# Rotary embedding of a sparse attention: swapping half heads by transfers within SBUF instead of by a permutation on TensorE

## The reference, cut to what matters

```python
def apply_rope(x):                 # x: (b, s, heads, 64)
    half = d // 2
    c, sn = jnp.cos(ang), jnp.sin(ang)
    x1, x2 = x[..., :half], x[..., half:]
    return jnp.concatenate([x1 * c - x2 * sn, x1 * sn + x2 * c], axis=-1)

def dsa_attention(xn, w_in, w_o):
    q, k, v, qi, ki, wi = jnp.split(xn @ w_in, A_SPLITS, axis=-1)
    q, k, qi, ki = apply_rope(q), apply_rope(k), apply_rope(qi), apply_rope(ki)
    ...                            # index scores, top 64 keys, softmax, values
    return from_blocks(o) @ w_o
```

## Time and profile before

| | us |
|---|---|
| median of 3 runs | 1352.4 (1350.19 to 1352.61) |
| profiled execution, its own time | 1350.53 |
| its span, first to last instruction | 1348.8 |
| TensorE busy | 1303.3 (97%) |
| VectorE, ScalarE, GpSimd busy | 948.8, 701.5, 128.3 |
| granted TensorE clock, mean | 0.998 |

### The profile page before, as it was taken

The page is one execution under the profiler, slowest core; times in us unless marked ns, Lnnn a source line. Parts: engine busy times, 40 slices in busy tenths (PEclk is TensorE's granted clock), DMA queues, the critical chain, the costliest instruction groups (busy, mean ns, idle before and its releaser), DMA issues. The chain is left out here.

```text
span 1348.8 us, 24952 instructions
## 1 busy us (share of the span) xinstructions
PE 1303.3 (97%) x10507; PEld 1129.8 (84%) x10507; DVE 948.8 (70%) x1433; ACT 701.5 (52%) x1211; POOL 128.3 (10%) x133
## 2 busy tenths in 40 slices
PE   4999999999999999999999999999999999999997
PEld 2998888998899897788888887888888998888886
DVE  1887788976768776675566888666656677756655
ACT  2544544434567555564444648654445566644443
POOL 0000000010200764100000042000000021000000
PEclk9999999999999999999999999999999999999999
DMA  9996799995341012356665532465555543565561
GB/s 362 372 363 237 299 356 380 352 343 167 115 156 64 4 35 97 95 176 201 188 189 176 182 113 91 148 206 192 187 190 160 174 139 126 172 188 194 183 197 50
DMA packets 177575, 256.90 MB, mean 190 GB/s; under 512 B 10488, under 2 KB 122552, under 8 KB 177464
## 3 DMA queue, kind: packets, MB, share of 16 engines
q1 hardware_dynamic: 177464, 255.31, 56.8%
HBM read 254.25 MB, written 1.05 MB: 189 GB/s over the span
## 5 line engine op out<-in xcount | busy, mean ns | idle before, releaser
L1514 DVE TENSOR_TENSOR w_lo<-stage,w_hi 128x1024 fp32r<-128x1024 f32 (+1 forms) x372 | 447.6, 1239 | 160.4 <-ACT w_hi L889 160.0
L889 ACT ACTIVATE w_hi<-stage 128x1024 fp32r<-128x1024 f32 (+1 forms) x378 | 380.1, 1049 | 211.7 <-PE acc L2318 191.9
L2316 PE MATMUL acc<-w_hi,z_hi 128*128 128x512 f32 x640 | 252.6, 395 | 1.6 <-DVE z_lo L1963 1.6
L2318 PE MATMUL acc<-w_hi,z_lo 128*128 128x512 f32 x640 | 249.4, 390 | 0.0
L2317 PE MATMUL acc<-w_lo,z_hi 128*128 128x512 f32 x640 | 249.2, 389 | 0.0
L2259 PE MATMUL un<-h_both,w_hi 128*128 128x256 f32 x736 | 214.3, 291 | 1.8 <-POOL w_lo L860 1.1
L2260 PE MATMUL un<-h_both,w_hi 128*128 128x256 f32 x736 | 208.1, 283 | 0.0
L2261 PE MATMUL un<-h_both,w_lo 128*128 128x256 f32 x736 | 208.0, 283 | 0.0
L2259 PEld LDWEIGHTS un<-h_both,w_hi 128*128 128x128 f32 x736 | 140.8, 191 | 9.5 <-issue 5.4
L2316 PEld LDWEIGHTS acc<-w_hi,z_hi 128*128 128x128 f32 x640 | 120.1, 188 | 27.8 <-issue 4.0
L2260 PEld LDWEIGHTS un<-h_both,w_hi 128*128 128x128 f32 x736 | 141.0, 192 | 1.2 <-issue 0.7
(11 more groups left out here) (393 smaller groups left out, 1886.0 us busy)
## 6 DMA issues: line engine op xcount, KB each, us to landing
stage<-in_mlp_w SPq DMA_DIRECT2D x64, 1024.0 KB
ada_buf<-in_ada_w SPq DMA_DIRECT2D x48, 1024.0 KB, 11.4
stage<-in_w_up SPq DMA_DIRECT2D x32, 1024.0 KB
stage<-in_w_down SPq DMA_DIRECT2D x32, 1024.0 KB
stage<-in_conv_w_in SPq DMA_DIRECT2D x12, 1024.0 KB
stage<-in_rw_w_rkv SPq DMA_DIRECT2D x12, 1024.0 KB
stage<-in_w_in_a SPq DMA_DIRECT2D x8, 1024.0 KB
stage<-in_w_kv_b SPq DMA_DIRECT2D x8, 1024.0 KB
```

The source lines that it names most:

```text
L889: A_(w_hi[u % 2][:, half, 0:n], stage[u % NSTAGE][:, half, 0:n], ACT.Copy).then_inc(hi_made, 1)
L1514: V.tensor_tensor(w_lo[u % 2][:, half, 0:n], stage[u % NSTAGE][:, half, 0:n], w_hi[u % 2][:, half, 0:n].bitcast(F32), ALU.subtract).then_i ...
L2316: MM(y, z_hi[:, kt, q], wh[:, i, :], start=(first and kt == 0), stop=False, skip_group_check=True)
L2318: ins = MM(y, z_lo[:, kt, q], wh[:, i, :], start=False, stop=(last and kt == KT - 1), skip_group_check=True)
```

## The change

The permutation leaves TensorE. Behind its copy to rope_in ScalarE waits until the copy is done (it waits on un_free, which the copy itself raises) and issues four transfers within SBUF, each of 32 partitions, which write the swapped halves to a buffer of their own, rope_turned (two of them). DVE waits for the transfers instead of for the matmul. The sign of the swapped half moves into the table of sines. The constant matrix is replaced by an unused one of the same size. PE no longer waits for a rotation before it writes the banks of the last two query units. The mask of the selection is waited for over another semaphore, in the same place.

```diff
-               (("ident", P), ("mean", P), ("ones", P), ("rot", P)),
+               (("ident", P), ("mean", P), ("ones", P), ("still", P)),
...
-    put("sin", np.tile(np.sin(ang), (4, 1)))
+    put("sin", np.tile(np.sin(ang), (4, 1)) * np.where(i % HD < HD // 2, -1.0, 1.0)[:, None])
...
+        rope_turned = [at(f"rope_turned{i}", [P, 2, SEQ], tmp_off + 4096 + 2048 * i) for i in range(2)]
...
                 A_(rope_in[r % 2][:, 0:n, :], un[v % 2][:, 0:n, :], ACT.Copy, scale=scale).then_inc(un_free, 1)
+                act.wait_ge(un_free, freed(v))
+                for g in range(4):
+                    to, src = 32 * g, 32 * (g ^ 1)
+                    act.dma_start(rope_turned[r % 2][to:to + 32, 0:n, :], rope_in[r % 2][src:src + 32, 0:n, :]).then_inc(sem(f"rope_landed{r % 2}"), 16)
...
-            def rope(r, n, dst, bank=misc):
-                dve.wait_ge(rot_done, r + 1)
-                link(V.tensor_tensor(dst, bank[:, 0:n, :], bc4(sin_root, n), ALU.mult))
+            def rope(r, n, dst):
+                dve.wait_ge(sem(f"rope_landed{r % 2}"), 64 * (r // 2 + 1))
+                link(V.tensor_tensor(dst, rope_turned[r % 2][:, 0:n, :], bc4(sin_root, n), ALU.mult))
...
-            dve.wait_ge(rot_done, ROPE_KI + 1)
+            dve.wait_ge(wi_turned, 1)
...
-            V.tensor_scalar(sel_bias[:], score[:], 0.5 * TAKEN, NEG, ALU.is_gt, ALU.mult).then_inc(sem("keys_chosen"), 1)
-            dve.wait_ge(sem("keys_chosen"), 1)
+            link(V.tensor_scalar(sel_bias[:], score[:], 0.5 * TAKEN, NEG, ALU.is_gt, ALU.mult))
...
-            def rot(r, n, v):
-                pe.wait_ge(un_free, freed(v))
-                if r:
-                    pe.wait_ge(rope_done, r)
-                MM(misc[:, 0:n, :], rot_w, rope_in[r % 2][:, 0:n, :], start=True, stop=True).then_inc(rot_done, 1)
...
-                if k >= 7:
-                    pe.wait_ge(rope_done, ROPE_Q + k - 6)
...
-            rot(ROPE_KI, 1, V_A)
+            ins.then_inc(wi_turned, 1)
             a_unit(2)
-            rot(ROPE_QI, 2, V_A + 1)
             a_half(3, 0)
-            rot(ROPE_QI + 1, 2, V_A + 2)
             a_half(3, 1)
             index_scores(0)
             a_half(4, 0, tokens=True)
-            rot(ROPE_K, 2, V_A + 3)
             index_scores(1)
...
-            rot_query(0)
...
-            rot_query(1)
...
-                if p in (1, 3):
-                    rot_query(p // 2 + 2)
```

More of the change, by code:

```diff
@@ L45 @@
            "c", "final_g", "g_attn_a_2", "g_kv_2", "g_attn_b_2", "g_mlp_2", "g_final_2")
-CONST_PARTS = ((("ident", P), ("mean", P), ("ones", P), ("rot", P)),
+CONST_PARTS = ((("ident", P), ("mean", P), ("ones", P), ("still", P)),
                (("head_ones", P), ("head_mean", P), ("level_t", 6 * CHUNK), ("masks", 2 * CHUNK), ("eye", CHUNK), ("resets", SEQ),
@@ L76, in constant_table @@
     put("head_mean", same_head / HD)
[L77 to L81, removed]
     s, q = i[:, None] % CHUNK, np.arange(CHUNK)[None, :]
@@ L167, in c_ @@
             return const[i][:, lo - CONST_AT[i]:hi - CONST_AT[i]]
-        ident, mean_w, ones_w, head_ones, head_mean, rot_w = (c_(n) for n in ("ident", "mean", "ones", "head_ones", "head_mean", "rot"))
+        ident, mean_w, ones_w, head_ones, head_mean = (c_(n) for n in ("ident", "mean", "ones", "head_ones", "head_mean"))
         level_t = c_("level_t").rearrange("p (j q) -> p j q", j=6)
@@ L726, in build @@
                              "bonus_gated", "weighed", "scaled", "group_done", "last_done"))
-        rot_done, rope_done, ki_copied, cos_done, kdup_ready = (sem(n) for n in ("rot_done", "rope_done", "ki_copied", "cos_done", "kdup_ready"))
+        wi_turned, rope_done, ki_copied, cos_done, kdup_ready = (sem(n) for n in ("wi_turned", "rope_done", "ki_copied", "cos_done", "kdup_ready"))
         score_done, score_relu, score_used = sem("score_done"), sem("score_relu"), sem("score_used")
@@ L2158, in rope_query @@
             def rope_query(j):
-                rope(ROPE_Q + j, 2, q_fm[:, 2 * j:2 * j + 2, :], un[(V_A + 5 + j) % 2])
+                rope(ROPE_Q + j, 2, q_fm[:, 2 * j:2 * j + 2, :])
             rope_query(0)
             select(rounds - rounds // 2)
-            V.tensor_scalar(sel_bias[:], score[:], 0.5 * TAKEN, NEG, ALU.is_gt, ALU.mult).then_inc(sem("keys_chosen"), 1)
-            dve.wait_ge(sem("keys_chosen"), 1)
+            link(V.tensor_scalar(sel_bias[:], score[:], 0.5 * TAKEN, NEG, ALU.is_gt, ALU.mult))
             pair_logits(0, 0)
@@ L2844, in a_half @@
                     free_bank(V_A + k)
-                    if k >= 7:
-                        pe.wait_ge(rope_done, ROPE_Q + k - 6)
                 unit(U_KI + k, un[(V_A + k) % 2], h_tiles, tokens=tokens, kts=HALVES[n])
-            def rot_query(j):
-                v = V_A + 5 + j
-                pe.wait_ge(un_free, freed(v))
-                MM(un[v % 2][:], rot_w, rope_in[(ROPE_Q + j) % 2][:], start=True, stop=True).then_inc(rot_done, 1)
             def a_products(p):
@@ L2874, in _ @@
             for a in range(QT):
-                nc.tensor.transpose(misc[:, 1, IDX_HEADS * a:IDX_HEADS * (a + 1)], rope_in[ROPE_KI % 2][HD:KI_COLS, 0, P * a:P * a + P],
+                ins = nc.tensor.transpose(misc[:, 1, IDX_HEADS * a:IDX_HEADS * (a + 1)], rope_in[ROPE_KI % 2][HD:KI_COLS, 0, P * a:P * a + P],
                                     ident[HD:KI_COLS, HD:KI_COLS])
-            rot(ROPE_KI, 1, V_A)
+            ins.then_inc(wi_turned, 1)
             a_unit(2)
-            rot(ROPE_QI, 2, V_A + 1)
             a_half(3, 0)
-            rot(ROPE_QI + 1, 2, V_A + 2)
             a_half(3, 1)
```

## The result

The changed kernel takes 1367.24 us in the median of six runs (1364.57 to 1371.98), the kernel before, run beside it, 1351.06 us (1349.97 to 1352.61). The ratio is 1.0123, its 95% interval 1.0100 to 1.0146: 16.2 us slower, where the forecast said 5.7, and above the upper end of its range (1363.5). Why the six runs lie 7.4 us apart was not found.

The account below looks back on a forecast made before the run. ACT and DVE, not the 97% busy PE, were taken to have least room; +3.0 us up to q0's addition and +2.7 at q3 made +5.7, on 1350.5 to 1352.4 us: 1357.5 us predicted, range 1352.5 to 1363.5.

Parts of the forecast that it names:

- block of 1.9 us: At every rotation: four transfer issues (1.81 us, taken from SyncE's rows) plus ACT's wait for its copy cost ACT 1.9 us.
- landing of 2.1 us: Time from a transfer's issue to its landing, taken from stores out of SBUF: 2.1 us, hidden at most rotations.
- Rival A: PE's time counts: the removed 7.1 us of PE work are gained, 1343.4 us (1345.3 on the median); chance 0.08.
- B: Rival: issues cost ACT next to nothing, +1.0 us at q3, sum 0, 1350.5 to 1352.4 us; chance 0.12.
- +3.7: First step, rotations KI and QI: ACT's issues delay splits k = 2 and 3, so DVE's tables begin 3.7 us later.
- Step 2, QI+1: Rotation QI+1: copy waits for KI's rotation until 774.8 us; PE's index scores start 3.2 us later, PE idle about 3 us.
- gain of 0.8 us at QI: Rotation QI: without the permutation, DVE's addition waits only for POOL's product and starts 0.8 us earlier.
- Step 4, q0: Rotation q0: copy 2.1 us later, then transfers and landing; DVE's addition starts at 802.45 instead of 799.48 us, +3.0.
- Rival C: Transfers land late, at 4.1 us, as weight loads share the DMA engines: +10.2 us, 1361 to 1363 us; chance 0.20.
- Step 6, q3: Last query rotation, q3: copy to addition takes 5.2 instead of 2.53 us, as issues and landing are exposed: +2.7 us.
- Rival D: PE's idle 3 us before the index scores lowers its clock: +3 to +4 us on top, 1361 us; chance 0.07.
- Steps 3 and 5, the hidden ones: K's issues cost 0 in ACT's wait for index scores (cover 1.9 us left); q1's and q2's transfers are hidden too.

## Why the prediction was wrong

It had the direction and the mechanism: PE's time doesn't count, ACT and DVE have the least room, waits appear ahead of the index scores and at q3. It was wrong in size, by a factor of nearly three. What failed are two terms that it sized too small, ACT's block of 1.9 us for each rotation (3.1 us at KI, 2.7 at QI) and the landing of 2.1 us (5.5 us at q0, 3.7 at q3), and one that it left out of the sum, the low clock behind q3 (2.5 us). Step by step:

*What bounds the kernel.* Right. The kernel without permutations and transfers is not faster (1.0012), and the page's 97% was no bound here. Rival A is dead. So is B: the transfers that nobody reads, and the half number of them, show that the issues are the larger part. The kernel without transfers shows one thing more that no rival had: PE's idle time at q3 alone brings the clock down, for 1.6 us.

*The block of 1.9 us.* Too small. The forecast took four issues for 1.81 us by the earlier trace rows, loads of lora_g2b from memory, "since it has the shape". The transfers within SBUF take 2.44 us at best, 2.85 us at KI and 3.54 us at q0, where one issue of the four is long. At KI and QI this alone turns +3.7 into +5.6. The upper bound was missing: the nearest rows were taken as value and a smaller one as lower end, with nothing above.

*Step 2, QI+1.* The forecast had its copy wait for KI's rotation until 774.8 us. That rotation ended at 776.9 us, as the tables were late, and the copy waited 0.5 us more for PE: unit 2, started 2.9 us late and computed at 0.50 and 0.65 of the clock, gave the bank up at 777.39 us. So 2.1 of the 3.7 us by which +6.9 exceeds +3.2 are the block's size again, 0.5 is PE's clock, and most of the rest is QI+1's own block ahead of split k = 4. With PE kept busy the copy waits for KI's rotation, as forecast, and the index scores are no sooner for it. The gain of 0.8 us at QI was 0.2, because "I take no difference" between PSUM and SBUF was wrong while POOL works. That PE stood idle about 3 us there (2.9), as forecast, is luck in part: both ends of the wait were late, by 3.7 us and more.

*Step 4, q0.* +3.0 was forecast at its addition; in the trace it has lost 5.5 us since its own copy. One issue of 1.69 us and a landing of 5.53 us beside a weight load did it. Rival C had a landing of 4.1 us at chance 0.20, and judged the mechanism rightly but too small and too rare: "loads come in bursts with pauses" was true, but a load starts when a unit has been split, and that is when the next bank is copied, so transfers and loads meet by the order of the lists.

*Step 6, q3.* Copy to addition 6.9 us, forecast 5.2, before 2.5. Landing 3.7 us instead of 2.1, issues 2.45 us. Alone it cost 6.3 us: 4.4 by the later addition, and 1.9 by PE's clock of 0.75 and 0.50 behind it. With the load held back copy to addition takes 5.2 us, the forecast's number, but by two errors that cancel: the issues take longer (2.45 for 1.81 us), and a landing counts from the start of the last issue and not from its end.

*The clock.* Rival D expected one low stretch ahead of the index scores; there are four in the attention, behind every long wait. Ahead of the index scores a low clock is a consequence and not a cause. Behind q3 it is a cause: 2.5 us in the changed kernel's trace, 1.9 with q3 alone, as PE's matmuls follow each other there with nothing left to wait for. Keeping the clock up gave back 0.9 to 1.5 us by the medians, within the noise, so for the whole kernel its share stays rough.

*Steps 3 and 5, the hidden ones.* Alone K and q1 cost 2.7 us; the cover of K's issues in the kernel before was 0.5 us, not 1.9. In the changed kernel, with index scores 6.9 us late, it is longer, so here the forecast's zero is nearer than the part suggests.

## What to carry to other kernels

A transfer that moves few bytes is paid in its issue (0.6 us of the issuing engine's list each) and its landing (2 us at best); count instructions, not bytes, and price them at more than the cheapest row nearby. Put the issues behind the work that others wait for, and look at what else reaches the DMA engines in those 2 us: the event that lets the small transfer go often also lets the next large load go. An operation of 0.9 us on an engine that seems full costs nothing as long as another engine releases it; taking it away gains nothing either, and the idle time that it leaves can bring the clock down ahead of a stretch that is PE's own. Issues that stand behind a long instruction run beside it; issues that must wait for one, and that the next one stands behind, do not.

## What the runs showed of the hardware

- Issues of transfers within SBUF take 0.61 us on ScalarE and 0.59 us on SyncE with 32 partitions, 0.56 us with 64; now and then one takes 0.9 to 1.7 us, on both engines. What makes these long was not found.
- With no weight load near, 64 KB within SBUF land 1.9 to 2.9 us after their issue; beside a 1 MB load, issued up to 2 us before or after them, mostly 3.7 to 6.7 us.
- ScalarE's issues of transfers run while it computes the instruction ahead of them (764.53 us beside w_hi of 764.40 to 765.45 us), if they need not wait for it.
- Products of DVE and POOL that both read SBUF slow each other: POOL 1.28 to 1.63 us, DVE 0.69 to 1.85 us.
- Behind 4 us in which PE had worked 0.76 us the granted clock was 0.50 (1.2 GHz) for the next 4 us and 0.65 for four more; behind the wait at q0 it took 12 us (0.55, 0.50, 0.67) to be back at 1.00 (2.4 GHz). The same stretch of matmuls behind q3 took 30.95 us at 1.00 and 32.6 to 34.6 us where the clock was low at its start.
